# Local attention in ten steps a block: value products two steps behind their tile, queries split in halves

## What is computed

```python
s_loc = einsum('bnqhgd,bnkhd->bnhgqk', qb, kw) * scale      # three blocks of 128 keys
s_loc = where(mask, s_loc, NEG_INF)
s_ctx = einsum('bnqhgd,blhd->bnhgql', qb, kc) * scale       # 256 context keys
p = softmax(concatenate([s_loc, s_ctx, s_sink], axis=-1))
o = einsum('bnhgqk,bnkhd->bnqhgd', p_loc, vw) + einsum('bnhgql,blhd->bnqhgd', p_ctx, vc)
...
y = concatenate([attn * silu(g_att), ...]) @ w_out
```

## Time and profile before

| | |
|---|---|
| median of 3 runs | 4971.81 us (4970.56 to 4973.96) |
| the profiled execution: time | 4970.33 us |
| the profiled execution: span | 4968.7 us |
| PE busy | 4091.6 us, 82% of the span |
| DVE busy | 2546.2 us, 51% |
| ACT busy | 1581.5 us, 32% |
| POOL busy | 1141.3 us, 23% |
| attention, tokens, layer 0 | from 920.8 us to about 1331 us of the span |
| attention, tokens, layer 1 | first POOL work of queries at 2178.21 us, last store issued at 2575.53 us |
| mean granted clock of PE | 0.904 |

### The profile page before, as it was taken

How to read it: one execution, slowest core, us unless ns; L and a number is a source line. 1 busy time by engine, 2 the same in 40 slices (tenths; PEclk the granted TensorE clock), 3 DMA queues, 4 the chain that set the end, 5 groups by cost and what they waited for, 6 DMA issues and landing times. The chain is left out here.

```text
span 4968.7 us, 50832 instructions
## 1 busy us (share of the span) xinstructions
PE 4091.6 (82%) x19014; PEld 3221.9 (65%) x19014; DVE 2546.2 (51%) x3304; ACT 1581.5 (32%) x2582; POOL 1141.3 (23%) x911
## 2 busy tenths in 40 slices
PE   7757998677689699868768969999998847776997
PEld 1446886665558588666555858877886636664776
DVE  1444763577623476357763654441000169995554
ACT  1233111465421311146642121232111255554331
POOL 0222110111121111011112111111110018885444
PEclk9978998788899799978879979999999969997999
DMA  7424121411252312141125231123121146554453
GB/s 299 161 74 161 60 81 63 108 43 43 78 176 98 122 50 90 63 106 45 43 73 180 94 123 72 68 98 116 70 76 64 72 138 155 147 139 150 172 176 104
DMA packets 307710, 527.88 MB, mean 106 GB/s; under 512 B 26239, under 2 KB 203031, under 8 KB 288345
## 3 DMA queue, kind: packets, MB, share of 16 engines
q1 hardware_dynamic: 272362, 364.87, 23.7%
q0 software_dynamic: 35136, 160.23, 8.6%
HBM read 372.02 MB, written 153.00 MB: 106 GB/s over the span
## 5 line engine op out<-in xcount | busy, mean ns | idle before, releaser
L457 PE MATMUL in_ps<-h,in_wp 128*128 128x512 f32 x6624 | 1510.2, 390 | 18.6 <-POOL in_wp L620 18.5
L457 PEld LDWEIGHTS in_ps<-h,in_wp 128*128 128x128 f32 x6624 | 1247.8, 188 | 281.0 <-POOL in_wp L620 21.3
L1620 PE MATMUL out_ps<-out_y,out_wp 128*128 128x512 f32 x3072 | 720.4, 396 | 74.4 <-ACT out_y L1514 34.9
L1620 PEld LDWEIGHTS out_ps<-out_y,out_wp 128*128 128x128 f32 x3072 | 584.2, 191 | 209.9 <-issue 64.0
L590 DVE SCALAR_TENSOR_TENSOR cy<-cu,in_cw,cy 128x2048 f32<-128x2048 f32 x120 | 314.5, 2621 | 4.3
L1553 POOL TENSOR_TENSOR out_wp<-out_w,out_wp 128x2048 fp32r<-128x2048 f32 (+1 forms) x48 | 193.0, 4025 | 421.3 <-ACT out_wp L1503 421.2
L518 ACT ACTIVATE in_ob<-in_ps 128x2048 f32<-128x2048 f32 x37 | 69.7, 1884 | 664.3 <-PE in_ps L457 664.3
L981 DVE TENSOR_TENSOR att_pT<-att_T,att_pT 128x512 fp32r<-128x512 f32 x320 | 221.1, 691 | 100.2 <-ACT att_pT L905 99.8
L620 POOL TENSOR_TENSOR in_wp<-in_w,in_wp 128x1024 fp32r<-128x1024 f32 x75 | 201.9, 2694 | 250.2 <-ACT in_wp L468 215.0
L960 DVE CUSTOM_DVE_ANT_0 att_S<-att_S,att_mk,att_nsink 128x640 f32<-128x640 f32 x256 | 226.7, 885 | 41.6 <-PE att_S L829 40.0
L671 DVE TENSOR_TENSOR hi_wp<-hi_w,hi_wp 128x512 fp32r<-128x512 f32 x8 | 4.9, 685 | 460.6 <-ACT hi_wp L691 460.6
(11 more groups left out here) (480 smaller groups left out, 6642.6 us busy)
## 6 DMA issues: line engine op xcount, KB each, us to landing
in_w<-in_w_in SPq DMA_DIRECT2D x75, 512.0 KB, 3.6
ada_w<-in_w_ada SPq DMA_DIRECT2D x18, 2048.0 KB, 9.5
gates<-in_ob POOLq DMA_DIRECT2D x36, 1024.0 KB, 4.2
out_w<-in_w_out SPq DMA_DIRECT2D x32, 1024.0 KB, 4.8
att_qf<-q SPq DMA_DIRECT2D x64, 256.0 KB, 4.4
out_yr<-y SPq DMA_DIRECT2D x16, 1024.0 KB, 7.8
x<-out_x POOLq DMA_DIRECT2D x64, 256.0 KB, 2.6
out_yr<-y SPq DMA_DIRECT2D x32, 512.0 KB, 5.7
```

Source lines behind the costliest of these rows:

```text
L457: mm = nc.tensor.matmul(ps[:, q, c * W:(c + 1) * W], wp[:, q, i, k], h[:, j, k, c * W:(c + 1) * W], start=(n + k == 0), stop=(n == 2 and k ...
L1620: mm = nc.tensor.matmul(ps[:, u % NB, :W], wp[:, u % NW, a, k], y[:, c % 2, b, k], start=(i + k == 0), stop=(i == 2 and k == KY - 1))
```

## The change

- `SL` is max(NH, U) = 10: a block has ten steps, and one table of `STEPS` = NB x SL + 4 steps runs through all blocks.
- `place(u)` gives tile u its place in the ring: the reciprocals' transpose (`RDEN`) now stands between tiles 8 and 9, the spreading product (`SPREAD`) behind tile 9.
- `valued(t)`: value products stay two steps behind their tile, but across the end of the block: those of tiles 8 and 9 are made in steps 0 and 1 of the next block. `cross` follows them in the same step on ACT, `add` one step later on DVE (steps 1 and 2 of the next block).
- `sum_up` and `invert` of a block move from the end of the block before to step 1 of the block itself. `shift` and `sink_exps` stand at the end of step 9.
- `query_heads` and POOL's `rest` work on halves (four heads each). For block b + 2 the first half is made in step 4 of block b, the second in step 9; before, all of it was made in step 8. `scores` waits for its half.
- SP's order of loads stays.

```diff
@@ -707,7 +707,8 @@
-    SL = max(NH, TU)
+    SL, LAG = max(NH, U), 2
+    STEPS = NB * SL + LAG + 2
@@ -736,6 +737,17 @@
+        def place(u):
+
+            return u if u < U - 1 else u + 1
+
+        RDEN, SPREAD = U - 1, U + 1
+
+        def valued(s):
+
+            b, u = divmod(s - LAG, SL)
+            return (b, u) if s >= LAG and u < U and b < NB else None
@@ -785,26 +797,29 @@
-            def rest(b):
-                pool.wait_ge(qled, b + 1)
-                pool.tensor_tensor(qs[HD:P, b % 2], qf[HD:P, b % 2], qs[HD:P, b % 2].bitcast(F32), ALU.subtract).then_inc(qparted, 1)
+            def rest(b, half):
+                pool.wait_ge(qled, 2 * b + half + 1)
+                part = slice(half * GQ, (half + 1) * GQ)
+                pool.tensor_tensor(qs[HD:P, b % 2, part], qf[HD:P, b % 2, part], qs[HD:P, b % 2, part].bitcast(F32), ALU.subtract).then_inc(qparted, 1)
...
             def turn_rden(b):
-                n = b * TU + U
+                n = b * TU + RDEN
                 pe.wait_ge(inverted, b + 1)
                 pe.wait_ge(freed, n - 1)
...
             def spread(b):
-                n = b * TU + U + 1
-                pe.wait_ge(freed, n)
+                n = b * TU + SPREAD
+                pe.wait_ge(freed, n - 1)
...
-            for b in range(NB):
-                for u in range(SL):
-                    if u < NH and b + 1 < NB:
-                        scores(b + 1, u)
-                    if u < U:
-                        turn(b, u)
-                    elif u == U:
+            for t in range(STEPS):
+                b, u = divmod(t, SL)
+                if u < NH and b + 1 < NB:
+                    scores(b + 1, u)
+                if u < U and b < NB:
+                    turn(b, u)
+                    if u == U - 2:
                         turn_rden(b)
-                    elif u == U + 1:
+                    if u == U - 1:
                         spread(b)
-                    if 2 <= u < U + 2:
-                        values(b, u - 2)
+                if valued(t):
+                    values(*valued(t))
...
+            for t in range(STEPS):
+                b, u = divmod(t, SL)
+                if u < U and b < NB:
+                    heads(b, u)
+                if u < NH and b + 1 < NB:
+                    exps(b + 1, u)
+                if b + 2 < NB and u in (4, SL - 1):
+                    query_heads(b + 2, 0 if u == 4 else 1)
+                if b + 1 < NB and u == SL - 1:
+                    sink_exps(b + 1)
+                if valued(t) and valued(t)[1] >= U - 2:
+                    cross(valued(t)[0], valued(t)[1] - (U - 2))
...
+            for t in range(STEPS):
+                b, u = divmod(t, SL)
+                if u < NH and b + 1 < NB:
+                    maxima(b + 1, u)
+                if 1 <= b < NB and u == 1:
+                    sum_up(b)
+                    invert(b)
+                if u < U and b < NB:
+                    rest(b, u)
+                    if u == U - 2:
+                        pick(b)
+                    if u == U - 1:
+                        scale_gate(b)
+                if valued(t - 1) and valued(t - 1)[1] >= U - 2:
+                    add(valued(t - 1)[0], valued(t - 1)[1] - (U - 2))
+                if b + 1 < NB and u == SL - 1:
+                    shift(b + 1)
```

More of the change, by code:

```diff
@@ L750, in queries @@
             def queries(b):
-                wait(sp, qparted, b - 1)
+                wait(sp, qparted, 2 * (b - 1))
                 for r in range(2):
@@ L802, in _ @@
             pool.wait_ge(const, 2)
-            rest(0)
-            rest(1)
+            for b in range(2):
+                for half in range(2):
+                    rest(b, half)
             for b in range(NB):
                 if b + 2 < NB:
-                    rest(b + 2)
+                    for half in range(2):
+                        rest(b + 2, half)
                 gate(b)
@@ L831, in turn @@
             def turn(b, u):
-                kt, g, n = u // 2, u % 2, b * TU + u
+                kt, g, n = u // 2, u % 2, b * TU + place(u)
                 if kt == 0:
@@ L841, in values @@
                 kt, g, r = u // 2, u % 2, (b * U + u) % 4
-                pe.wait_ge(freed, b * TU + u + 1)
+                pe.wait_ge(freed, b * TU + place(u) + 1)
                 if kt == 0:
@@ L882, in key_heads, with query_heads @@
                 nc.scalar.activation(kA[:, :, c0:c1], kf[:, :, c0:c1], ACT.Copy).then_inc(kled, 1)
-            def query_heads(b):
+            def query_heads(b, half):
                 act.wait_ge(q_in[b % 2], 32 * (b // 2 + 1))
-                wait(act, scored, (b - 1) * NH)
-                nc.scalar.activation(qs[:, b % 2], qf[:, b % 2], ACT.Copy).then_inc(qled, 1)
+                wait(act, scored, (b - 2) * NH + (half + 1) * GQ)
+                part = slice(half * GQ, (half + 1) * GQ)
+                nc.scalar.activation(qs[:, b % 2, part], qf[:, b % 2, part], ACT.Copy).then_inc(qled, 1)
             def exps(b, hh):
@@ L892, in exps @@
                 if hh == 0:
-                    wait(act, turned, (b - 2) * TU + U)
+                    wait(act, turned, (b - 2) * TU + place(U - 1) + 1)
                 nc.scalar.activation(prob[:, b % 2, hh], psS[:, n % 2, S0:S0 + NK], ACT.Exp, bias=nm[:, b % 2, hh:hh + 1], scale=-1.0,
@@ L901, in heads @@
             def heads(b, u):
-                n, m = b * TU + u, b * U + u
+                n, m = b * TU + place(u), b * U + u
                 act.wait_ge(turned, n + 1)
@@ L925, in _ @@
                 key_heads(p)
-            for b in range(NB):
-                for u in range(SL):
-                    if u == 0 and b >= 1:
-                        cross(b - 1, 1)
-                    if u < U:
-                        heads(b, u)
-                    if u < NH and b + 1 < NB:
-                        exps(b + 1, u)
-                    if u == min(NH, SL - 1):
-                        if b + 1 < NB:
-                            sink_exps(b + 1)
-                        if b + 2 < NB:
-                            query_heads(b + 2)
-                    if u == SL - 1:
-                        cross(b, 0)
-            cross(NB - 1, 1)
+            for t in range(STEPS):
[10 more added lines that the diff above has]
+                    cross(valued(t)[0], valued(t)[1] - (U - 2))
         @block.vector
@@ L974, in invert @@
                 dve.wait_ge(summed_up, b + 1)
-                wait(dve, turned, (b - 2) * TU + U + 1)
+                wait(dve, turned, (b - 2) * TU + RDEN + 1)
                 nc.vector.reciprocal(rden[:, b % 2], den[:, b % 2]).then_inc(inverted, 1)
             def rest(b, u):
-                n, m = b * TU + u, b * U + u
+                n, m = b * TU + place(u), b * U + u
                 dve.wait_ge(led, m + 1)
@@ L1020, in _ @@
             invert(0)
-            for b in range(NB):
-                for u in range(SL):
-                    if b >= 1 and u < 2:
-                        add(b - 1, u)
-                    if u < NH and b + 1 < NB:
-                        maxima(b + 1, u)
-                    if u < U:
-                        rest(b, u)
-                    elif u == U:
+            for t in range(STEPS):
[8 more added lines that the diff above has]
+                    if u == U - 2:
                         pick(b)
-                    elif u == U + 1:
+                    if u == U - 1:
                         scale_gate(b)
-                    if b + 1 < NB:
-                        if u == min(NH, SL - 1):
-                            shift(b + 1)
-                        if u == min(NH + 1, SL - 1):
-                            sum_up(b + 1)
-                        if u == min(NH + 2, SL - 1):
-                            invert(b + 1)
-            add(NB - 1, 0)
-            add(NB - 1, 1)
+                if valued(t - 1) and valued(t - 1)[1] >= U - 2:
+                    add(valued(t - 1)[0], valued(t - 1)[1] - (U - 2))
+                if b + 1 < NB and u == SL - 1:
+                    shift(b + 1)
 def fourier(nc, name, N, u_d, tab_d, headtab_d, wf_d, bf_d, gate_d, out_d):
```

16 lines of the change are left out of this document (9 added, 7 removed).

## The result

The changed kernel takes **4888.86 us** (median of 4 runs, 4885.11 to 4892.09), the kernel before 4972.18 us (4 runs beside it). The ratio is 0.9832, 95% interval 0.9815 to 0.9849: faster by 1.7%. Forecast were 4877 us and a range from 4842 to 4915.

The account below looks back on a forecast made before the run. Waits at block hand-overs (10.27 of 23.73 us) were taken to bound the attention stages. Hand-over 4.66, steps 14.6 and clock 1.05 gave 20.4 us; 28 x 3.3 plus context, 93 us, off 4970.3: 4877 us, range 4842 to 4915.

Parts of the forecast that it names:

- Hand-over 4.66 us: Block end, from remainder 7's end to the next block's first maximum: 4.66 us in place of 10.27.
- the turn of the ring: Block end: two shared transposed tiles set the pace from remainder 8 to remainder 9, 2.02 us.
- Steps 0 to 7, 14.6 us: First eight steps of a long-stage block: 13.56 us of Vector's work, 14.6 us with PE's new wait.
- the accumulator's wait: Step 2: value product 0 waits 1.5 us for the previous block's addition; 0.6 us for the other half.
- twice the wait: Upper bound for steps 0 to 7 if the accumulator's wait doubles: 15.9 us.
- Who is held: Vector against POOL: the sum, moved to step 1, loses 1.16 us; the shift is held 0.45 us by POOL's second half.
- A fall in every second block: Block end: PE drops to 1.2 GHz in every second block, 2.1 us each, 1.05 us per block on the mean.
- Half of it brings 1.2 us: Context stage: its first scores wait for POOL's remainder, so halving that brings 1.2 us.
- The clock stays up: Rival, long stages: PE's idle before the spreading product is gone, so no falls; 4846 us, chance 0.12.
- A fall in every block: Rival, block ends: the clock falls every time, 4905 us; with the new wait twice as long 4942; chance 0.14.
- PE didn't stay at 1.2 GHz: Judges the slower rival: PE at 1.2 GHz in all long-stage steps, blocks 29.5 us, 5132 us, chance 0.03.
- the ring of two tiles: Rival, block end: two transposed tiles shared by four keep the old hand-over; about 4970 us, chance 0.02.

Follow-up runs that it names:

- the additions first: Changed kernel with Vector's two additions of halves moved ahead of sum, reciprocal and remainders in steps 1 and 2: 4854.03 us; with unused products as well, 4839.23 us.
- the added products: Changed kernel plus unused PE products per hand-over, 5 behind tile 8 and 3 behind the value products of step 8: 4850.76 us.
- shift moved: Changed kernel with the unused products and the shift moved from step 9 to step 8, directly behind the pick: 4853.83 us.
- the best kernel: Changed kernel plus unused products at block ends and in each attention stage's last block, additions ahead of the sum, shift in step 8, halves kept: 4838.32 us.

## Why the prediction was right, and where it wasn't

**Hand-over 4.66 us: right to the hundredth**, in a block without a fall. The stretch up to remainder 8 was counted 0.81 us and took 0.79 (1018.04 to 1018.83), the turn of the ring 2.02 and 2.07 (1018.83 to 1020.90), the rest 1.83 and 1.80. So the mechanism was right term by term; the last hundredth is luck, small errors that cancel.

**Steps 0 to 7, 14.6 us: right in size, but one term of it wrong.** 19.25 - 4.66 = 14.6. The count put 1.0 us above Vector's own work down to the accumulator's wait. The wait is there (1.27 us where 1.5 was counted, 0.4 for the other half where 0.6), but with it out of the way only 0.41 us is saved. The other 0.6 is not that wait: with the additions first and the clock up, steps 0 to 7 still take 18.84 - 4.66 = 14.2 us against 13.56 of Vector's own work. In that trace 0.37 us of it is one wait of Vector for Scalar's copy, in step 5; the rest comes in pieces of about 0.1 us or less. (The count's upper bound, 15.9 us for "twice the wait", doesn't follow from it either: 1.5 + 0.6 more would be 16.7.)

**Who is held.** The sum is free at 0.16 us, as counted. The shift, counted at 0.61, is held at 28 of 28 hand-overs: 0.40 to 0.68 us, and 0.66 to 0.68 in all of them where the added products keep the clock up. From its start to the next instruction it is 0.59 above. POOL's half in the timeline ends with it:

```profile
1021.47 1.28 POOL L803 TENSOR_TENSOR att_qs<-att_qf,att_qs 64x512 fp32r<-64x512 f32 x1 [6.18 <-ACT att_qs L904]
```

1021.47 + 1.28 = 1022.75, and the shift of above ends at 1022.11 + 0.67 = 1022.78. By the Trainium skill ("SBUF — State Buffer", section "Who interferes with whom") where two such instructions meet, the one that issues second is blocked until the first is through. The trace agrees: POOL's half starts 0.64 us ahead of the shift, and both end together. What the hold costs was mis-sized, in one sentence of the forecast: without it "the time would be 28 x 0.45 = 13 us less". The count itself had the first scores ready 3.7 us behind the start of remainder 8, and Vector with the hold at 3.85, so only 0.15 could be saved. Measured are 3.74 (1051.27 to 1055.01, shift moved) and 3.87, and a gain of 0.12.

**Clock: right in kind, near in size, and that by luck.** A fall in every second block at 2.1 us, 1.05 on the mean, was forecast. Measured are 9 falls in 15 hand-overs; over 13 blocks of layer 0 they add 15.9 us, 1.22 a block. But "every second block" was the middle between never and always; no row gave it. The kernels beside this one had 0, 3, 9 and 25 falls in 30, so small edits decide it. The two sizes go with how long 1.2 GHz lasts. Behind the pick of a block of 20.6 us the clock is back within a few us, behind that of a block of 21.6 us it stays at 0.50 for 3.5 us more.

**Sum of the long stages**: 92 us were forecast, 93.7 measured.

**Context's stage: the step that failed.** "Half of it brings 1.2 us" was forecast, since the first scores wait for POOL's remainder. With the halves alone the first score product does come 1.1 us sooner in the stage (at 8.91 us for 10.02), but the stage is only 0.18 us shorter: the wait wasn't on its path. With the whole change it takes 2.4 us more. The trace of the kernel before, POOL's gating of the two blocks and the spreading product of the second:

```profile
339.44 1.28 POOL L797 TENSOR_TENSOR attc_o<-attc_sm,attc_gR 128x512 f32<-128x512 f32 x1 [17.11 <-DVE attc_sm L999]
346.76 1.25 POOL L797 TENSOR_TENSOR attc_o<-attc_sm,attc_gR 128x512 f32<-128x512 f32 x1 [4.95 <-DVE attc_sm L999]
```

```profile
343.51 1.12 PE L860 MATMUL attc_T<-attc_dR,attc_gsel 8*128 8x512 f32 x2 [0.71 <-DVE attc_dR L986]
```

and of the changed one:

```profile
338.43 1.26 POOL L810 TENSOR_TENSOR attc_o<-attc_sm,attc_gR 128x512 f32<-128x512 f32 x1 [15.62 <-DVE attc_sm L1013]
351.15 1.25 POOL L810 TENSOR_TENSOR attc_o<-attc_sm,attc_gR 128x512 f32<-128x512 f32 x1 [10.36 <-DVE attc_sm L1013]
```

```profile
344.80 2.07 PE L876 MATMUL attc_T<-attc_dR,attc_gsel 8*128 8x512 f32 x2
```

The stage starts 1.97 us later than before, so the first block is 3.0 us sooner by the stage's own time; the second comes 12.72 us behind it, in place of 7.32. Three pairs of value products now stand behind the spreading product, where one pair stood before, and all of them run at 1.2 GHz. With added products there (the best kernel) the spreading product and the last gating are

```profile
342.97 1.12 PE L887 MATMUL attc_T<-attc_dR,attc_gsel 8*128 8x512 f32 x2
```

```profile
347.38 1.25 POOL L810 TENSOR_TENSOR attc_o<-attc_sm,attc_gR 128x512 f32<-128x512 f32 x1 [7.96 <-DVE attc_sm L1029]
```

and the stage is 2.2 us shorter. From the start of the spreading product to that of the last gating are 3.25 us before (343.51 to 346.76), 6.35 in the changed kernel and 4.41 here. So of the 3.1 us by which this tail grew, 1.9 are the clock's and 1.2 the order's, in a stage for which the forecast looked at neither. Even at 2.4 GHz the new order only breaks even there (41.79 us for 41.61). The size has some noise: with the old order and no added product in it, the stage took 43.24 us in one kernel, where PE's clock rose 3.2 us later at its start. The ten kernels with the new order and no added products in this stage take 43.5 to 44.9.

**The rest.** From one profiled execution to the other the gain is 4970.33 - 4892.09 = 78.2 us, 15.1 short of the forecast's 93.3. Of these the context's stage makes 3.6, the long stages -1.7, and 13.0 are in stages whose instructions are the same; the median lies 3.2 below the profiled execution. In the profiles of the twelve other kernels those stages take 1.2 to 11.5 us more than in the one of before. Part of it is that the one profile of before is the lowest of all; which stages move changes from one to the next (the stage behind the first attention by 4.1 us in this one and -0.4 with the additions first). What moves them stays open.

**The rivals.** "The clock stays up" (4846 us, 0.12) fell; made true by the added products, it gives 4850.76. The Trainium skill ("TensorE: Matmul & The Clock Gate", part 1, "A second HAM failure mode: psum-queue depth-cycling") tells of a kernel in which short idle times between groups of matmuls came often enough to make the clock swing between its two levels. The traces agree: 18 falls with no wait of PE over 1.27 us. "A fall in every block" (4905 us) is nearest to what the order alone with whole queries shows: 25 falls in 30 hand-overs, but at some 1.0 us each, so 4884 us. PE didn't stay at 1.2 GHz, and the ring of two tiles didn't keep the old hand-over.

## What to carry to other kernels

Where the clock falls at some hand-overs and not at others, small edits elsewhere in the block can decide how often. Here two moved lines, which changed a wait in step 2 and the length of the block, took half of the falls at the block's end away; in the new order that was worth more than the split of the queries. A hold or a wait is worth only what stands behind it without cover; read the next instruction's releaser before counting it. A place that is free of a hold in one kernel need not be in the next: the shift in step 8 was free with halved queries and held for 2.0 us with whole ones. And a schedule made for many blocks has to be read once more in the stage that has two.

## What the hardware showed that wasn't expected

The clock fell where PE was busy 1.84 of the 2.41 us before and had no idle over 0.84 us in them. The fall is also not tied to an instruction. In the kernel with the new order and whole queries, whose blocks are all alike, the mean granted clock over the 2.5 us from 1 us behind the pick is, at the hand-overs of blocks 0, 5 and 9 of layer 0:

```profile
983.95:986.45 2.50, 2.50 (x6) 1.23 (x6) 1.36 (x3) 0.64 (x2) 1.73 (x1) 0.61 0.00 0
1085.25:1087.75 2.50, 2.21 (x6) 1.02 (x6) 1.36 (x3) 0.65 (x2) 1.76 (x1) 0.83 0.00 0
1166.70:1169.20 2.50, 2.21 (x7) 1.01 (x7) 1.36 (x3) 0.69 (x2) 1.80 (x1) 0.93 0.00 0
```

In the 3.5 us behind these windows the clock is meanwhile lower each time (0.79, 0.63, 0.57). So the fall comes a little later in each block, and in block 12 it doesn't come at all. And three unused products of 384 columns at each hand-over (20.8 us of PE's time for all 90, 0.69 for three) took all 18 falls of the two layers away.
